# The last token product's second half as two chains of 256 columns, and the last tile's normalisation on three engines

## What is computed

```python
# mix = concat(pooling mixer, mLSTM) @ w_out, then:
x1 = LayerNorm(ALPHA * x + mix) * ln1_g + ln1_b
ff = square(relu(x1 @ w_ff1 + b_ff1)) @ w_ff2 + b_ff2     # 1024 -> 4096 -> 1024
y  = LayerNorm(ALPHA * x1 + ff) * ln2_g + ln2_b           # over the 1024 channels of a token
```

## Time and profile before

| | us |
|---|---|
| median of 3 runs (1053.29 to 1053.95) | 1053.66 |
| the profiled execution, its own time | 1053.76 |
| the profiled execution, its span in the trace | 1052.0 |
| PE busy | 1040.9 |
| DVE busy | 719.1 |
| ACT busy | 486.8 |
| POOL busy | 87.8 |

### The profile page before, as it was taken

The page is one execution under the profiler, slowest core; times in us unless marked ns, Lnnn a source line. Parts: engine busy times, 40 slices in busy tenths (PEclk is TensorE's granted clock), DMA queues, the critical chain, the costliest instruction groups (busy, mean ns, idle before and its releaser), DMA issues. The chain is left out here.

```text
span 1052.0 us, 18890 instructions
## 1 busy us (share of the span) xinstructions
PE 1040.9 (99%) x7797; PEld 1028.0 (98%) x7797; DVE 719.1 (68%) x956; ACT 486.8 (46%) x685; POOL 87.8 (8%) x120
## 2 busy tenths in 40 slices
PE   9999999999999999999999999999999999999997
PEld 9999999999899999999999999999999999999985
DVE  6795675536786595855655655658766677887977
ACT  6554434445533576644554554556443323334223
POOL 3111321020211000000000000000000000000027
PEclk9999999999999999999999999999999999999999
DMA  8543988365224211254345345387524425325304
GB/s 281 144 175 93 227 226 153 91 164 125 86 86 152 90 41 55 78 167 156 120 154 166 110 150 171 121 276 261 207 82 148 174 62 182 121 92 171 122 5 157
DMA packets 95154, 148.34 MB, mean 141 GB/s; under 512 B 6164, under 2 KB 51956, under 8 KB 94568
## 3 DMA queue, kind: packets, MB, share of 16 engines
q1 hardware_dynamic: 88290, 127.72, 38.2%
q0 software_dynamic: 6528, 19.19, 8.1%
q10 hardware_dynamic: 270, 0.49, 0.2%
HBM read 104.19 MB, written 49.06 MB: 146 GB/s over the span
## 5 line engine op out<-in xcount | busy, mean ns | idle before, releaser
L2340 PE MATMUL bank<-x_hi,w_hi 128*128 128x344 f32 (+1 forms) x696 | 227.5, 327 | 0.2 <-DVE x_lo L1616 0.2
L2340 PE MATMUL bank<-x_hi,d_lo 128*128 128x258 f32 x968 | 222.4, 282 | 0.0
L2340 PE MATMUL bank<-x_lo,w_hi 128*128 128x344 f32 (+1 forms) x696 | 222.0, 319 | 0.0
L2340 PE MATMUL bank<-x_hi,w_lo 128*128 128x344 f32 x528 | 168.7, 319 | 0.0
L2340 PEld LDWEIGHTS bank<-x_hi,d_lo 128*128 128x128 f32 x968 | 165.7, 189 | 0.0
L2340 PEld LDWEIGHTS bank<-x_hi,w_hi 128*128 128x128 f32 (+1 forms) x696 | 130.4, 187 | 0.9 <-DVE x_lo L1616 0.5
L2340 PEld LDWEIGHTS bank<-x_lo,w_hi 128*128 128x128 f32 (+1 forms) x696 | 130.2, 187 | 0.4
L2340 PE MATMUL bank<-x_lo,s_hi 128*128 128x258 f32 x448 | 126.5, 282 | 0.0
L2340 PE MATMUL bank<-x_hi,s_hi 128*128 128x258 f32 x448 | 126.4, 282 | 0.0
L2340 PEld LDWEIGHTS bank<-x_hi,w_lo 128*128 128x128 f32 x528 | 99.2, 188 | 0.0
L2340 PE MATMUL bank<-t_hi,s_hi 128*128 128x258 f32 x336 | 95.2, 283 | 0.0
(11 more groups left out here) (400 smaller groups left out, 2433.8 us busy)
## 6 DMA issues: line engine op xcount, KB each, us to landing
h_ops<-h_unit SPq DMA_DIRECT2D x56, 258.0 KB, 2.5
x_lo_raw<-h_ops SPq DMA_DIRECT2D x14, 1032.0 KB, 5.2
s_raw<-in_w_ff SPq DMA_DIRECT2D x14, 1024.0 KB, 6.9
x_lo_raw<-h_ops SPq DMA_DIRECT2D x14, 774.0 KB, 4.5
d_raw<-in_w_ff SPq DMA_DIRECT2D x9, 1024.0 KB, 7.3
w_raw<-in_w_in SPq DMA_DIRECT2D x16, 512.0 KB, 7.8
h_ops<-t_out SPq DMA_DIRECT2D x28, 258.0 KB, 5.2
d_raw<-in_w_ff SPq DMA_DIRECT2D x8, 768.0 KB, 6.4
```

Source lines behind the costliest of these rows:

```text
L2340: return nc.tensor.matmul(out, lhsT, rhs, start=start, stop=stop, skip_group_check=True)
```

## The change

The changed kernel alters the end of the program alone.

- PE: `y_T(8)` is cut into two calls of 4 transposes, one ahead of each half of tile 8. The second four, and the second half's product, go to a new place, `LAST_HALF`: columns 0 to 255 of banks 4 and 5. They wait until ACT has read tile 5 out of those banks (`l2_norm` at 12). The second half is made as two chains of 12 matmuls of 256 columns (`token_quarter`), each with its own count on `l2_T`.
- DVE: tile 8 gets four `bn_stats` of 256 columns in place of two of 512, one `bn_aggr` over their 24 numbers, and two centrings of 512 columns in place of one of 1024: the first half, then (behind the reciprocal) the second. Then DVE scales and adds the bias for the second half only, in two `scalar_tensor_tensor` of 256 columns. The four sets of statistics lie across columns that tile 6 and tile 7 used, so DVE waits for ACT's activations of tile 6 first.
- ACT: `l2_scaled(8, 256)`, two activations of 256 columns for the first half. Its queue then stores 120 rows of the third and of the fourth quarter (120 KB each), and then the 8 sample rows, which wait for POOL.
- POOL: two adds of 256 columns for the first half.
- SP: in place of the sample rows it stores the 120 rows of the first half (240 KB) once POOL has added both quarters.

```diff
+        LAST_HALF = two[2][:, :, 0:256]
@@ sync
-            sp.wait_ge(l2_last, 2)
-            sp.dma_start(a["y_sample"][:, 0, :], OUT[2][SEQ - L2T[8][0]:L2T[8][1], :]).then_inc(out_done[2], 16)
+            t0 = L2T[8][0]
+            sp.wait_ge(l2_b, 10)
+            sp.dma_start(a["y_prompt"][0, t0:SEQ, 0:512], OUT[2][0:SEQ - t0, 0:512]).then_inc(out_done[2], 16)
             for s in range(3):
-                sp.wait_ge(out_done[s], 48 + 32 * (s == 2))
+                sp.wait_ge(out_done[s], 48 + 48 * (s == 2))
@@ gpsimd
+            n = L2T[8][1]
+            for q in range(2):
+                cs = slice(256 * q, 256 * (q + 1))
+                pool.wait_ge(l2_norm, 2 * 8 + q + 1)
+                G.tensor_tensor(OUT[2][0:n, cs], OUT[2][0:n, cs], GB[0:n, 1, cs], ALU.add).then_inc(l2_b, 1)
@@ scalar
             l2_root(8)
-            t0 = L2T[8][0]
-            for half in range(2):
-                cs = slice(512 * half, 512 * (half + 1))
-                act.wait_ge(l2_last, half + 1)
+            l2_scaled(8, 256)
+            t0, n = L2T[8]
+            for q in (2, 3):
+                cs = slice(256 * q, 256 * (q + 1))
+                act.wait_ge(l2_last, q - 1)
                 act.dma_start(a["y_prompt"][0, t0:SEQ, cs], OUT[2][0:SEQ - t0, cs]).then_inc(out_done[2], 16)
+            act.wait_ge(l2_b, 10)
+            act.dma_start(a["y_sample"][:, 0, :], OUT[2][SEQ - t0:n, :]).then_inc(out_done[2], 16)
@@ vector
-            for t in (7, 8):
-                ln2_first_half(t)
...
+            ln2_first_half(7)
...
             n = L2T[8][1]
-            dve.wait_ge(l2_g, 9 - N_NORMED)
+            x, z = bank[L2_BANK[8]][0:n, :], LAST_HALF[0:n, :, :]
+            quarters = LNT[0:n, :, :].rearrange("p q c -> p (q c)")
+            dve.wait_ge(l2_norm, 2 * 7)
+            dve.wait_ge(l2_stats, 2 * 8)
+            for q in range(4):
+                dve.wait_ge(l2_T, (10, 10, 11, 12)[q])
+                last = V.bn_stats(quarters[:, 6 * q:6 * q + 6], x[:, 256 * q:256 * (q + 1)] if q < 2 else LAST_HALF[0:n, q - 2, :])
+            last.then_inc(l2_stats, 1)
+            dve.wait_ge(l2_stats, 2 * 8 + 1)
+            V.bn_aggr(LNT[0:n, 2, 12:14], quarters[:, 0:24]).then_inc(l2_stats, 1)
+            dve.wait_ge(l2_stats, 2 * 8 + 2)
+            stt(x, x, LNT[0:n, 2, 12:13], GB[0:n, 0, 0:512], ALU.subtract, ALU.mult).then_inc(l2_g, 1)
+            ln2_scale(8)
+            stt(z, z, LNT[0:n, 2, 12:13], halves(GB[0:n, 0, 512:1024]), ALU.subtract, ALU.mult).then_inc(l2_g, 1)
+            dve.wait_ge(l2_g, 10 - N_NORMED)
             dve.wait_ge(l2_numbers, 2 * N_NORMED + 9 - N_NORMED)
             dve.wait_ge(out_done[2], 32)
-            for half in range(2):
-                stt(OUT[2][0:n, 512 * half:512 * (half + 1)], bank[L2_BANK[8] + half][0:n, :], LNT[0:n, 2, 16:17],
-                    GB[0:n, 1, 512 * half:512 * (half + 1)], ALU.mult, ALU.add).then_inc(l2_last, 1)
+            for q in (2, 3):
+                cs = slice(256 * q, 256 * (q + 1))
+                stt(OUT[2][0:n, cs], z[:, q - 2, :], LNT[0:n, 2, 16:17],
+                    GB[0:n, 1, cs], ALU.mult, ALU.add).then_inc(l2_last, 1)
@@ tensor
+            def token_quarter(t, quarter):
+                ts = slice(L2T[t][0], L2T[t][0] + L2T[t][1])
+                half, cs = quarter // 2, slice(256 * (quarter % 2), 256 * (quarter % 2 + 1))
+                o = LAST_HALF[0:L2T[t][1], quarter % 2, :]
+                for k in range(FG // P):
+                    mm(o, HH[:, k, ts], W2H[half][:, k, cs], False, False)
+                    mm(o, HH[:, k, ts], W2L[half][:, k, cs], False, False)
+                    last = mm(o, HL[:, k, ts], W2H[half][:, k, cs], False, k == FG // P - 1)
+                last.then_inc(l2_T, 1)
...
-            y_T(8)
+            y_T(8, range(0, 4))
             token_product(8, 0)
-            token_product(8, 1)
+            y_T(8, range(4, KC))
+            for quarter in (2, 3):
+                token_quarter(8, quarter)
```

More of the change, by code:

```diff
@@ L1340, in l2_normed, with l2_scaled @@
                       bias=LNT[0:n, q, 17:18], scale=LNT[0:n, q, 16:17]).then_inc(l2_norm, 1)
-            def l2_scaled(t):
+            def l2_scaled(t, w=512):
                 n, q = L2T[t][1], t % 3
@@ L1346, in l2_scaled @@
                 act.wait_ge(out_done[t % 3], 16 * (t // 3))
-                for half in range(2):
-                    A(OUT[t % 3][0:n, 512 * half:512 * (half + 1)], bank[L2_BANK[t] + half][0:n, :], ACT.Copy,
+                for part in range(2):
+                    cs = slice(w * part, w * (part + 1))
+                    A(OUT[t % 3][0:n, cs], bank[L2_BANK[t] + part][0:n, :] if w == 512 else bank[L2_BANK[t]][0:n, cs], ACT.Copy,
                       scale=LNT[0:n, q, 16:17]).then_inc(l2_norm, 1)
@@ L2322, in _ @@
                 ln2_scale(t)
-            for t in (7, 8):
-                ln2_first_half(t)
-                ln2_second_half(t)
-                ln2_centred_gain(t)
-                ln2_scale(t)
-            n = L2T[8][1]
-            dve.wait_ge(l2_g, 9 - N_NORMED)
+            ln2_first_half(7)
+            ln2_second_half(7)
+            ln2_centred_gain(7)
+            ln2_scale(7)
+            n = L2T[8][1]
+            x, z = bank[L2_BANK[8]][0:n, :], LAST_HALF[0:n, :, :]
[13 more added lines that the diff above has]
+            dve.wait_ge(l2_g, 10 - N_NORMED)
             dve.wait_ge(l2_numbers, 2 * N_NORMED + 9 - N_NORMED)
             dve.wait_ge(out_done[2], 32)
-            for half in range(2):
-                stt(OUT[2][0:n, 512 * half:512 * (half + 1)], bank[L2_BANK[8] + half][0:n, :], LNT[0:n, 2, 16:17],
-                    GB[0:n, 1, 512 * half:512 * (half + 1)], ALU.mult, ALU.add).then_inc(l2_last, 1)
+            for q in (2, 3):
+                cs = slice(256 * q, 256 * (q + 1))
+                stt(OUT[2][0:n, cs], z[:, q - 2, :], LNT[0:n, 2, 16:17],
+                    GB[0:n, 1, cs], ALU.mult, ALU.add).then_inc(l2_last, 1)
         @block.tensor
@@ L2767, in sum_T, with y_T @@
                 last.then_inc(l2_T, 1)
-            def y_T(t):
+            def y_T(t, chunks=range(KC)):
                 t0, n = L2T[t]
@@ L2776, in y_T @@
                     pe.wait_ge(l2_norm, 10)
-                for f in range(KC):
-                    nc.tensor.matmul(bank[L2_BANK[t] + f // 4][0:n, P * (f % 4):P * (f % 4 + 1)], Y[:, f, t0:t0 + n], IDN[:, :],
-                                     start=f % 4 == 0, stop=False, is_transpose=True, skip_group_check=True)
+                for f in chunks:
+                    o, first = bank[L2_BANK[t] + f // 4][0:n, P * (f % 4):P * (f % 4 + 1)], f % 4 == 0
+                    if t == 8 and f >= 4:
+                        if f == 4:
+                            pe.wait_ge(l2_norm, 12)
+                        o, first = LAST_HALF[0:n, f // 2 - 2, P * (f % 2):P * (f % 2 + 1)], f % 2 == 0
+                    nc.tensor.matmul(o, Y[:, f, t0:t0 + n], IDN[:, :], start=first, stop=False, is_transpose=True, skip_group_check=True)
             def token_product(t, half):
```

## The result

The changed kernel takes 1055.88 us (median of 22 runs, 1055.19 to 1058.74) against 1053.90 for the kernel before (22 runs): 2.0 us slower, ratio 1.0020 with a 95% interval of 1.0014 to 1.0026. The forecast was 1053.3, no measurable change, in a range up to 1054.2. The profiled execution of the changed kernel took 1056.70, its span is 1054.7, so 2.7 longer than the 1052.0 of before.

A forecast was written before the change was run, and what follows sets the result against it. PE, busy 99%, and the 7.9 us behind its last matmul were taken as the bound. PE +0.09, arithmetic to the last large issue -0.29, landing -0.2 gave -0.4 from 1053.66: 1053.3 us, range 1052.6 to 1054.2.

The forecast's parts named there:

- a closing of 1.3: End of the span: 1.3 us following SP's wait for the last stores, 1050.7 to 1052.0, left unchanged.
- Rival 4: First-half branch's end: POOL's add mostly fixed cost, gain gone at 0.87 us an add, 2.1 us loss at 1.9; chance 0.02.
- The term for POOL's add: First half of the last tile: each POOL add of 256 columns takes 0.67 us, two end at 1047.80.
- DVE and ACT: Behind the last matmul: statistics 0.43, scaling 0.48, centring of 512 columns 0.75, aggregation 0.21, ACT's activation 0.45 us.
- PE: Last tile's split transposes and 256-column matmuls: last result 0.09 us later; new waits cost nothing.
- The landing: Last stores: landed 2.5 us after the last large issue, at 1050.3, 0.4 earlier than before.
- the worst case of the stores: Last stores' landing: 1050.7, no gain; up to 0.3 us later if 1 KB rows cost more than half of 2 KB rows.
- case 2 of the rivals: Last stores: the DMA engines' drain decides, not the issues; 1053.6 to 1053.9 us, chance 0.22.
- The sum of 2.0 us and 436 GB/s: Store landing: fixed time per DMA plus transfer rate; 2.56 us for the last 240 KB, close to the forecast's 2.5.
- The Trainium skill's rule to coalesce: Last stores: by this rule, the case to expect was the DMA drain deciding, 1053.6 to 1053.9 us.
- "same" at 0.96: Whole kernel: time within 0.2% of before, chance 0.96; faster by more 0.01, slower by more 0.03.

The follow-up runs named there:

- c1: Kernel before with tile 7's scaling and bias on DVE, last tile's prompt rows in one SP store, sample rows by ACT's queue: 1054.06 us, ratio 1.0004.
- e2: Kernel before plus a wait of POOL for DVE's last scaling, with no operation behind it: 1056.05 us, ratio 1.0018.
- e1: Kernel before plus a one-column memset on POOL behind DVE's last scaling: 1055.96 us, ratio 1.0019.

## Why the prediction was wrong, step by step

- **The step that failed** is the closing: "a closing of 1.3 that follows SP's wait and that I leave as it is". It followed POOL's end, and the chain from POOL's last add to the end of the span is 5.8 + 0.2 us long. The record was there to be read: POOL's drain of 8353 ns from 1043.4, ending 5.81 behind the last add at 1045.95 and 0.75 behind SP's. With it the forecast's own times give the result: POOL's adds were to end at 1047.80, in place of 1045.95, 1.85 later; the measured difference of the medians is 1.98. Rival 4 had the right place, POOL's branch, and the wrong price: not a fixed part of the add but of the engine's end. It had 0.02; that 1055.9 lies inside its bounds is luck, since the adds took 0.72 and not 1.9.
- **The term for POOL's add** was right: 0.67 forecast, 0.68 as pitch and 0.72 as record. The estimate of 0.8 came from the 4497 ns that the Trainium skill (GPSIMD Engine Reference, Elementwise — side-by-side cycle accounting) gives for an add of 2048 columns; the measurement lies between, nearer to the memsets' line.
- **DVE and ACT**: 0.43 forecast and 0.42, 0.48 and 0.48, 0.75 and 0.74 to 0.76, 0.45 and 0.47; only the aggregation of 24 numbers took 0.26 and not 0.21 to 0.23. SP's last issue 3.69 behind the last matmul, forecast 3.63.
- **PE**: 0.09 forecast, 0.06 measured. Neither of the new waits on PE or DVE held anything up.
- **The landing** was mis-sized too, and this was hidden behind POOL: forecast 2.5 from the last large issue, measured 3.3 (SP's store from 1048.71 to 1052.0, the end of SP's wait; the view names the sample rows, issued at 1048.91, as what it waited for last). So even without POOL's end the change does not gain: its profile has SP's drain 7.20 behind the last matmul against 6.88, the other two with four stores 0.1 to 0.2 behind the others. That is the worst case of the stores ("up to 0.3 later"), at or just past the end of case 2 of the rivals. No run separates the fourth DMA from the rows of 1 KB or the order of the queues, so the cause stays open. The sum of 2.0 us and 436 GB/s in the Trainium skill (DMA: Bandwidth & Descriptors, Anatomy of one DMA) is a fit for DMAs issued from GpSimd, and these stores went out from the queues of SP and ACT; the prediction did not say so, and the sum was no measure for them. Taken for 240 KB it gives 2.56, an estimate, and this trace shows 0.7 more. The Trainium skill's rule to coalesce (same page, Rules for kernel authors) is meant for many small transfers, under 64 KB above all. These were of 240 KB, and c1, which joined two of them, lost 0.7 at SP's drain.
- **The chances**: "same" at 0.96 rested on cases that all ended with SP. That the change is small against 0.2% was true of the work it moves, not of what hangs on the engine to which it was moved.

## What to carry to other kernels

The engine that ends last is not always the one with the last work: read the closing barrier's records, for every engine, before costing a change at the end of a kernel. In a kernel like this one, whose GpSimd issues many DMAs, its part must be over early, by 0.08 us for each DMA that it has issued in the whole launch. Once it is the engine that ends last, helper work on it, even a wait, is paid in full, while the same loads from another engine's queue cost nothing at the end that these profiles show. Here, giving tile 7's last step to an idle DVE, taking 11 loads from POOL's queue, or both, puts the medians 0.6 to 0.9 under the kernel before. Each of the four measurements has an interval that just includes no gain; all four point the same way.

## What the runs showed of the hardware

- In this kernel POOL's drain at the end of the launch lasts 0.0815 us for each DMA issued by POOL and 0.08 more, whenever it was issued and whatever its size (4 KB or 512 KB): 4.91, 5.62, 5.79 and 7.42 us for 59, 68, 70 and 90. The added 20 were issued from 338 to 347 us, 700 us before the end; the 11 taken away had stood at the start (2 to 6 us) and at 991 us. SP's drain takes 0.013 us, with 239 DMAs of its own in the kernel before. What POOL does in that time the trace does not show.
- That time counts from when POOL's last operation is over and its sequencer has come to the drain; a wait without an operation delays it as work does (with the bare wait of e2 and with the memset of e1 the record lasts 5.785 alike).
- A store of 120 rows of 4 KB, with 8 more rows from a second queue, landed 3.5 us after its issue (c1), one of 128 rows of 4 KB in 2.6. The cause stays open.
